# Three differential heads: two probability maps joined by VectorE, then transposed and multiplied once

## The reference, cut to what matters

```
s = einsum("bqhmd,bkhmd->bhmqk", q_blk, k) * HEAD_DIM ** -0.5
s = s - slopes * dist ; s = where(dist >= 0, s, -inf)
p = softmax(s, axis=-1)
p_diff = p[:, :, 0] - lam * p[:, :, 1]
out = einsum("bhqk,bkhe->bqhe", p_diff, v)      # v is 128 wide
out = rms_norm(out, subln_g) * (1.0 - lambda_init)
```

## Time and profile before

| | us |
|---|---|
| median of 3 runs | 779.57 (778.48 to 781.56) |
| profiled execution, device time | 778.44 |
| its span, first to last instruction | 776.5 |
| mean granted TensorE clock | 0.997 |

### The profile page before, as it was taken

How to read it: one execution, slowest core, us unless ns; L and a number is a source line. 1 busy time by engine, 2 the same in 40 slices (tenths; PEclk the granted TensorE clock), 3 DMA queues, 4 the chain that set the end, 5 groups by cost and what they waited for, 6 DMA issues and landing times.

```text
span 776.5 us, 17043 instructions
## 1 busy us (share of the span) xinstructions
PE 762.2 (98%) x6010; PEld 735.3 (95%) x6010; DVE 585.0 (75%) x1061; ACT 448.4 (58%) x752; POOL 238.0 (31%) x147
## 2 busy tenths in 40 slices
PE   8999999999999999999999999999999999999996
PEld 8999999999999999999998989999999999988885
DVE  6899976768888887345876785779999999963333
ACT  7554556466656565445845665776666666653431
POOL 0376653463221220432580001622221222122220
PEclk9999999999999999999999999999999999999999
DMA  8466553555555567554443233345555555665551
GB/s 286 160 214 196 188 176 126 188 190 195 184 190 188 189 227 234 180 162 142 156 144 113 104 110 110 136 136 189 191 188 189 189 189 189 216 196 198 185 181 55
DMA packets 37773, 135.48 MB, mean 174 GB/s; under 512 B 4448, under 2 KB 4704, under 8 KB 37728
## 3 DMA queue, kind: packets, MB, share of 16 engines
q1 hardware_dynamic: 37728, 134.86, 52.3%
HBM read 133.80 MB, written 1.05 MB: 174 GB/s over the span
## 4 chain that ended last, share of the span: by engine, by line
PE 88%; DVE 4%; ACT 3%; issue 2%; DMA 1%; POOL 1%; SPq 0%; DVEq 0%; POOLq 0%; ACTq 0%
PE bank L1666 24%; PE bank L1667 23%; PE bank L1668 23%; PE bank L2013 4%; PE bank L2015 4%; PE bank L2014 4%; DVE w_lo L1059 2%; ACT w_hi L719 1%; DMA raw<-in_w_in 1%; PE bank L1881 1%; PE bank L1880 1%; PE bank L1688 1%; PE bank L1890 1%; DVE bank L1108 0%; PE bank L1736 0%
## 5 line engine op out<-in xcount | busy, mean ns | idle before, releaser
L1666 PE MATMUL bank<-h_hi,w_hi 128*128 128x256 f32 x1424 | 401.4, 282 | 4.3 <-DVE w_lo L1059 1.1
L1667 PE MATMUL bank<-h_lo,w_hi 128*128 128x256 f32 x1424 | 397.5, 279 | 0.0
L1668 PE MATMUL bank<-h_hi,w_lo 128*128 128x256 f32 x1424 | 397.3, 279 | 0.0
L719 ACT ACTIVATE w_hi<-raw 128x1024 fp32r<-128x1024 f32 (+2 forms) x244 | 260.3, 1069 | 92.4 <-PE bank L1668 43.8
L1059 DVE TENSOR_TENSOR w_lo<-raw,w_hi 128x1024 fp32r<-128x1024 f32 (+2 forms) x177 | 225.0, 1273 | 100.8 <-ACT w_hi L719 100.7
L574 POOL TENSOR_TENSOR w_lo<-raw,w_hi 128x1024 fp32r<-128x1024 f32 (+1 forms) x67 | 166.0, 2480 | 363.9 <-ACT w_hi L719 363.8
L1666 PEld LDWEIGHTS bank<-h_hi,w_hi 128*128 128x128 f32 x1424 | 267.6, 188 | 10.5 <-issue 5.6
L1667 PEld LDWEIGHTS bank<-h_lo,w_hi 128*128 128x128 f32 x1424 | 267.7, 188 | 0.0
L1668 PEld LDWEIGHTS bank<-h_hi,w_lo 128*128 128x128 f32 x1424 | 267.6, 188 | 0.0
L1108 DVE TENSOR_TENSOR bank<-bank,scales 128x256 f32<-128x256 f32 x124 | 52.8, 429 | 27.1 <-PE bank L1668 13.2
L1336 DVE TENSOR_TENSOR f_lo<-src,f_hi 128x256 f32 (+1 forms) x54 | 58.5, 1084 | 0.5 <-ACT f_hi L867 0.5
(11 more groups left out here) (209 smaller groups left out, 921.0 us busy)
## 6 DMA issues: line engine op xcount, KB each, us to landing
raw<-in_w_up SPq DMA_DIRECT2D x108, 512.0 KB, 3.3
raw<-in_w_in SPq DMA_DIRECT2D x54, 512.0 KB, 3.5
raw<-in_w_down SPq DMA_DIRECT2D x32, 512.0 KB, 3.8
raw<-in_w_down SPq DMA_DIRECT2D x16, 704.0 KB, 4.2
raw<-in_w_o SPq DMA_DIRECT2D x8, 512.0 KB, 3.4
raw<-in_w_gate SPq DMA_DIRECT2D x8, 512.0 KB, 3.3
raw<-in_w_out SPq DMA_DIRECT2D x8, 512.0 KB, 3.3
raw<-in_w_b_out SPq DMA_DIRECT2D x4, 512.0 KB, 3.6
```

The costliest lines, as they stand in the source:

```text
L719: nc.scalar.activation(hi_of(u)[:, cols], raw[s][:, cols], ACT.Copy).then_inc(hi_ready, 1)
L1666: nc.tensor.matmul(ps, wh, hi[:, k, :], start=start and n == 0, stop=False)
L1667: nc.tensor.matmul(ps, wh, lo[:, k, :], start=False, stop=False)
L1668: last = nc.tensor.matmul(ps, wl, hi[:, k, :], start=False, stop=stop and n == len(ks) - 1)
```

## The change

For the heads in `JOINED` (0, 1 and 2) the two maps are made into one in SBUF. In the step after its exponentials DVE forms the denominators of the map and multiplies its first part's probabilities in place (`join`, 128x128 and 128x256); for the second part it multiplies by the second denominator (with minus `lam`) and adds the first map, again in place, and counts `join_done`. PE then transposes only the second map of such a head, now waiting for `join_done` where it waited for `exp_done`, and makes one value product. The output needs no scaling any more: ACT copies it from PSUM into `y_b` (`joined_output`). Head 3 keeps the old way. The counts in the waits follow from the tables `RUN` and `Y_DONE`.

```
+JOINED = (0, 1, 2)
+def joined(m):
+    return MAPS[m][0] == "diff" and MAPS[m][1] in JOINED
...
     for m in range(N_MAPS):
-        steps[m + 3]["score"], steps[m + 4]["trans"], steps[m + 5]["pv"] = m, m, m
+        steps[m + 3]["score"] = m
+        if joined(m):
+            steps[m + 4]["join"] = m
+        if not joined(m) or MAPS[m][2]:
+            steps[m + 4]["trans"], steps[m + 5]["pv"] = m, m
...
+            def joined_output(m):
+                h = MAPS[m][1]
+                act.wait_ge(pv_done, RUN[m])
+                nc.scalar.activation(y_b[:, :, P * h:P * (h + 1)],
+                                     pv_ps[:, 0:TOK].rearrange("p (b n) -> p b n", b=2), ACT.Copy
+                                     ).then_inc(y_done, 2)
...
+                if step["pv"] is not None and joined(step["pv"]):
+                    joined_output(step["pv"])
                 if step["v_trans"] is not None:
                     copy_v(step["v_trans"])
...
+            def join(m):
+                h, part = MAPS[m][1:]
+                denominators(m)
+                dve.wait_ge(den_done, DEN[m])
+                for b, (lo, hi) in enumerate(block_cols(m)):
+                    p = score[:, m % N_SWA, lo:hi]
+                    if part == 0:
+                        nc.vector.tensor_scalar(p, p, rden[:, m, b:b + 1], None, ALU.mult
+                                                ).then_inc(first_scaled, 1)
+                    else:
+                        dve.wait_ge(first_scaled, 2 * JOINED.index(h) + b + 1)
+                        nc.vector.scalar_tensor_tensor(p, p, rden[:, m, b:b + 1],
+                                                       score[:, (m - 1) % N_SWA, lo:hi],
+                                                       ALU.mult, ALU.add).then_inc(join_done, 1)
...
+                if step["join"] is not None:
+                    join(step["join"])
                 for tile, unit in step["copies"]:
                     copy_out(tile, unit)
...
-                if step["trans"] is not None:
+                if step["trans"] is not None and not joined(step["trans"]):
                     denominators(step["trans"])
-                if step["pv"] is not None:
+                if step["pv"] is not None and not joined(step["pv"]):
                     scaled_output(step["pv"])
...
             def transposes(m):
-                pe.wait_ge(exp_done, 2 * (m + 1))
+                if joined(m):
+                    pe.wait_ge(join_done, 2 * JOINED.index(MAPS[m][1]) + 2)
+                else:
+                    pe.wait_ge(exp_done, 2 * (m + 1))
```

More of the change, by code:

```diff
@@ L97 @@
 OUT2_SIDE = (4, 5)
+SWA_ORDER = [h for j in range(4) for h in (j, j + 4)]
+MAPS = [("swa", h, 0) for h in SWA_ORDER] + [("diff", h, m) for h in range(4) for m in range(2)]
+JOINED = (0, 1, 2)
+def joined(m):
+    return MAPS[m][0] == "diff" and MAPS[m][1] in JOINED
+RUN, Y_DONE = [], []
+for _m, (_kind, _, _part) in enumerate(MAPS):
+    _own = not (joined(_m) and _part == 0)
+    RUN.append((RUN[-1] if RUN else 0) + _own)
+    Y_DONE.append((Y_DONE[-1] if Y_DONE else 0) + 2 * _own)
 def make_steps():
     steps = [dict(unit=u if u < len(IN2_TILES) else None, copies=[], v_trans=None, score=None,
-                  trans=None, pv=None, y_sum=None, y_scale=None, y_chunks=[], out2=None)
+                  trans=None, join=None, pv=None, y_sum=None, y_scale=None, y_chunks=[], out2=None)
              for u in range(23)]
@@ L220 @@
 SLOPES = alibi_slopes(SWA_HEADS + DIFF_HEADS)
-SWA_ORDER = [h for j in range(4) for h in (j, j + 4)]
-MAPS = [("swa", h, 0) for h in SWA_ORDER] + [("diff", h, m) for h in range(4) for m in range(2)]
 DEN = []
@@ L468, in build @@
         den_done = sem("den_done")
+        first_scaled, join_done = sem("first_scaled"), sem("join_done")
         trans_done = sem("trans_done")
@@ L959, in copy_prob_T @@
             def copy_prob_T(m):
[L960 to L963, removed]
-                                     ).then_inc(probT_done, 1)
+                n = RUN[m]
+                act.wait_ge(trans_done, n)
+                if n > 2:
+                    act.wait_ge(pv_done, n - 2)
+                nc.scalar.activation(prob_T[(n - 1) % 2][:], probT_ps[:, 0:3 * P], ACT.Copy
+                                     ).then_inc(probT_done, 1)
+            def joined_output(m):
[4 more added lines that the diff above has]
+                                     ).then_inc(y_done, 2)
             def y_squares(i):
-                act.wait_ge(y_done, 2 * (8 if i == 0 else 8 + 2 * i))
+                act.wait_ge(y_done, Y_DONE[7 if i == 0 else 7 + 2 * i])
                 for b in range(2):
@@ L1482, in denominators @@
                                         ALU.mult).then_inc(den_done, 1)
+            def join(m):
[12 more added lines that the diff above has]
+                                                       ALU.mult, ALU.add).then_inc(join_done, 1)
             def scaled_output(m):
                 kind, h, part = MAPS[m]
-                dve.wait_ge(pv_done, m + 1)
+                dve.wait_ge(pv_done, RUN[m])
                 dve.wait_ge(den_done, DEN[m])
@@ L1499, in scaled_output @@
                         else:
-                            dve.wait_ge(y_done, 2 * m)
+                            dve.wait_ge(y_done, Y_DONE[m - 1])
                             nc.vector.scalar_tensor_tensor(y, pv, rden[:, m, b:b + 1], y, ALU.mult,
@@ L1884, in transposes @@
             def transposes(m):
-                pe.wait_ge(exp_done, 2 * (m + 1))
+                if joined(m):
+                    pe.wait_ge(join_done, 2 * JOINED.index(MAPS[m][1]) + 2)
+                else:
+                    pe.wait_ge(exp_done, 2 * (m + 1))
                 source = pieces(m)
                 if m >= 1:
-                    pe.wait_ge(probT_done, m)
+                    pe.wait_ge(probT_done, RUN[m] - 1)
                 for n in range(3):
@@ L1900, in value_product @@
                 pe.wait_ge(v_ready, 1 if kind == "swa" else h + 2)
-                pe.wait_ge(probT_done, m + 1)
+                pe.wait_ge(probT_done, RUN[m])
                 if m >= 1:
-                    pe.wait_ge(y_done, 2 * m)
-                pt = prob_T[m % 2]
+                    pe.wait_ge(y_done, Y_DONE[m] - 2)
+                pt = prob_T[(RUN[m] - 1) % 2]
                 nc.tensor.matmul(pv_ps[:, 0:width], pt[:, 0:P], v[:, 0, cols], start=True, stop=True)
@@ L1931, in out2_part @@
                     if i == OUT2_SIDE[0]:
-                        pe.wait_ge(probT_done, N_MAPS)
+                        pe.wait_ge(probT_done, RUN[-1])
                     elif i == OUT2_SIDE[1]:
-                        pe.wait_ge(y_done, 2 * N_MAPS)
+                        pe.wait_ge(y_done, Y_DONE[-1])
                     else:
```

## The result

| | us |
|---|---|
| before, median of 4 runs | 779.68 (778.48 to 781.56) |
| changed, median of 4 runs | 785.52 (783.56 to 786.44) |
| ratio, 95% interval | 1.0072 (1.0054 to 1.009) |
| profiled execution of the changed kernel, device time, span | 783.56, 781.6 |

The change makes the kernel 0.7% slower.

A forecast was written before the change was run, and what follows sets the result against it. PE, busy 98% of the span, was taken to bound the kernel. Stalls of 6.51 us less 3.28 of work gone put it 3.2 us late, forecasting 782.8 us from a median of 779.57, range 778.0 to 786.0.

The forecast's parts named there:

- the likeliest case: Whole kernel: PE stalls of 6.51 us less 3.28 us of work gone, clock holding; 782.8 us, 60%.
- same: Outcome within half a per cent (3.9 us) of before, neither below 775.7 nor above 783.5 us; chance 0.63.
- Work gone from PE, 3.28 us: Steps 12 to 17: maps 8, 10 and 12 lose their transposes and value products on PE, 3.28 us.
- The join, 1.42 us from mean square to transposes: DVE, second parts: mean square's start to PE's transposes takes 1.42 us, between 1.31 and 1.58.
- The place of the join, behind a mean square that waits for ACT: DVE, steps 13 and 15: the join stands behind mean squares that had waited 1.29 and 0.65 us for ACT's squares.
- The three heads: Transposes of maps 9, 11, 13: PE stalls 2.03, 2.02 and 2.46 us, ending 3.2 us late at map 13.
- The clock: Rival: PE's clock falls to 0.50 in the stalls, 1.7 us each; one fall 784.5 us, three 787.9; 19%.
- the partly hidden joins: Rival: shorter wait behind the squares or shorter products remove a third or more of the stalls; 779.5 to 781.5 us, 12%.
- The later fall that might move: Idle products behind the attention may miss their clock fall, giving back about 1 us: 781.8; no chance of its own.
- The other side's rival: All three joins are over when PE comes, so the 3.28 us saving comes through: 776.3 us, 7%.

The follow-up runs named there:

- e1: Changed kernel without the join: first maps of heads 0 to 2 and scaling of the second left out, output wrong; 777.26 us, 0.996 of before.
- e3: Changed kernel with DVE's mean square behind the join instead of ahead of it; 781.95 us, 1.0023 of before.
- e10: Changed kernel with only head 2 joined; 782.81 us, 1.0031 of before.
- e5: Changed kernel with PE's scores of the next map ahead of the transposes in steps 13, 15 and 17; 780.52 us, 1.0016 of before.
- e8: The changed kernel measured again, unaltered; 785.41 us, 1.0076 of before.
- e9: Changed kernel with only heads 0 and 1 joined; 783.30 us, 1.0034 of before.
- e2: Changed kernel with 8 idle products of 128 columns on PE ahead of each wait for the join; 782.76 us, 1.0038 of before.
- e4: Changed kernel with only head 0 joined; 780.93 us, 1.0016 of before.
- e6: Changed kernel with mean square behind join, scores ahead of transposes, map 13's join ahead of DVE's weight unit; 777.59 us, 0.9977 of before.
- e7: Changed kernel with mean square behind join, scores ahead of transposes, map 13's join earlier, and head 3 joined too; 780.05 us, 1.0005 of before.

## Why the prediction came out as it did

The time, 785.52, lies inside the range of 778.0 to 786.0 by half a microsecond, and two of the four executions lie above it. It is 2.7 above the 782.8 of the likeliest case and 1.2 above that case's upper end; the change is slower by more than half a per cent, which had 0.32 against 0.63 for "same". The range held because it had been drawn to take in one fall of the clock. The stalls were worked out well, and what the likeliest case left out is the clock.

**Work gone from PE, 3.28 us:** nearly right. By the transposes of map 13, e1 had gained 3.03 without a wait, and 2.90 at the end, with the new wait of 0.21 in between.

**The join, 1.42 us from mean square to transposes:** measured 1.34. The 256-wide product takes 0.48 where I took 0.47, and the two products together 0.75 where I took 0.73; it is PE that started 0.06 behind them (443.00 - 442.94) and not 0.15. The Trainium skill, page "VectorE: DVE Perf Modes", section on the TRN2 errata, gave an estimate of 0.33 for the 256-wide product; the same section says that its fixed term of 58 cycles is too small and that about 150 were measured, from which an estimate is 0.42. Both are shorter than the 0.48 measured here, and the row of L1150 was the better guide. The changed kernel's group of the joins on DVE (count | busy us, mean ns of one | idle time before them):

```profile
L1527 DVE SCALAR_TENSOR_TENSOR score<-score,rden 128x256 f32<-128x256 f32 x3 | 1.4, 480 | 0.0
```

**The place of the join, behind a mean square that waits for ACT:** right, and shown by e3, in which this one line moved takes 1.44 and 0.80 us off the first two waits. It is not the whole of the loss: e3 is still 0.23% above before; the third join is late by DVE's own work, and the clock still falls behind it.

**The three heads:** the kernels stand 0.64 us apart at the first scores of map 8 (432.61 and 431.97). Less that, the transposes of maps 9, 11 and 13 come at 442.36, 453.84 and 465.39; predicted 442.34, 453.88 and 465.36. PE's lateness, the distance to the kernel before at the same transposes, is 0.95, 1.82 and 3.26 us against 0.93, 1.86 and 3.2. The agreement to a few hundredths is in part luck. At map 9, for one, the scores came 0.10 us later than worked out (437.08 - 0.64 = 436.44, against 436.34), and the join was 0.08 shorter. The waits on the timeline, 1.78, 1.65 and 2.24, are shorter than the 2.0, 2.0 and 2.5 forecast; they are counted from the modelled end of PE's last product, which lies behind the start that the next one could have had, and PE also came a little later than worked out. e10 checks the third head by itself: the same working gives 463.50 for map 13, and it came at 464.00 - 0.49 = 463.51.

**The clock:** this is the step that failed. I gave a fall in the stalls 19% and kept it out of the sum, arguing that "these stalls are 2 us of silence in every 11, with dense work between, and 0.7 us left the clock alone". The wait of 0.7 said nothing on stalls three times as long. The row that bore on it more nearly was the fall after the stretch of 2.37 busy in 3.20 us, much of it on one-column products; the stretch around the third wait has 1.17 busy in 3.20. Falls in this stretch stand in the profiles of changed, e3, e5 and e8 behind the third wait (2.24, 2.17, 1.74 and 2.24 us), of e9 behind the second (1.65) and of e10 behind its only one (2.22); none stands in e1, e2, e4 (a wait of 1.78), e6 and e7 (1.96).

What a fall costs can be read from PE's lateness. In the changed kernel it grew from 3.26 at map 13 to 4.62 us at the transposes of 470.74, by 1.4, where the prediction had 1.7, half of 3.4. From the last joined map to the end of the second half a fall of 3.4 us added 1.3 in the changed kernel and 1.6 in e9, the 6.8 us of e3 and e10 added 2.9, and in e2 and e4, without a fall, nothing was added. So one fall was priced nearly right; that there may be two in a row was not foreseen. In the medians the clock cost about 2.7 us (changed less e2), as much as the likeliest case missed by; in single falls, an estimate from the 1.4 us of one, that is two in a usual execution.

The Trainium skill, page "TensorE: Matmul & The Clock Gate", Part 1, has the clock halve when PE has idled. The traces agree in kind: PE went from 1.00 to 0.50 behind waits of 1.65 to 2.24 us, and e2, which fills them, stayed at 1.00.

**Slips of the prediction:** the likeliest case's bounds add up to 782.5 to 783.6, and with half a microsecond of scatter on either side to 782.0 to 784.1, not 781.5 to 784.3. In the case of the partly hidden joins a third of the stalls, 2.2 us, gives 780.6, so its upper end of 781.5 is too high. And the profile of before has a second fall of the clock, from about 775.5 us on, behind PE's last product, where it costs nothing. None of the three changes the account.

**The later fall that might move:** it did in this profile (idle products 2.17 us for 3.76), and brought little, because PE then waited 0.70 for DVE's `h_lo`. The second half is 4.55 longer, the lead before it 0.64, and the span 5.1.

**The other side's rival:** hidden joins would have given 776.3. e1, which has no join to wait for, gives 777.26, and e6, in which the joins are nearly hidden, 777.59. So the saving is real, and it hangs on where the join stands.

## What to carry to other kernels

Where one engine bounds, work moved off it pays only if what it then waits for is done by the time at which it now arrives; read from the trace what the producer's queue is waiting for just ahead of the place where the new work will stand. Here a saving of about 3.0 us became a loss of 3.3 before any fall of the clock. A 0.17 us mean square that waited for a third engine made up 2.2 us of the waits (e3); DVE's own late turn and PE's order made up the most of the rest, and moving all three made the change a gain of 0.23% (e6). And price an idle gap of TensorE above its length: filling the gaps with idle products, which save no wait, gave back about 2.7 us in the medians.

## What the runs showed of the hardware

Falls of TensorE's granted clock to 0.50 stood behind single waits of 1.65 to 2.24 us in a stretch otherwise dense. They lasted some 3.4 us (changed kernel, e5, e8, e9) or 6.8 us (e3, e10), and not every such silence brought one: the changed kernel's first two, of 1.78 and 1.65 us, left the clock alone in both of its profiles, and in e7 a wait of 1.96 us did too. How busy PE was around the wait does not sort them either: in 3.2 us around it PE was busy for 1.17 us (third wait of the changed kernel) and 1.55 (e9) where a fall followed, and for 1.42 and 1.55 (first and second wait of the changed kernel) and 1.24 (e7) where none did. What decides between them, and why the length doubles, stays open.
